# Row norm of the first products applied at their evictions, rotary tables made in place, key halves split step by step

## The reference

```python
xn = rmsnorm(x, norm_mix_g[l])
proj = jnp.einsum('bsd,de->bse', xn, w_in[l])
q_lat, kv_lat, k_rope, dq, dk, dv, gate_pre = jnp.split(proj, split_idx, axis=-1)
...
k_pe = apply_rope(k_rope[:, :, None, :], positions, MLA_ROPE_DIM)
...
o_mla = causal_attention(q_mla, k_mla, v_mla).reshape(B, S, MLA_WIDTH)
dq = apply_rope(dq.reshape(B, S, DIFF_HEADS, 2, DIFF_HEAD_DIM), positions, DIFF_ROT_DIM)
dk = apply_rope(dk.reshape(B, S, DIFF_HEADS, 2, DIFF_HEAD_DIM), positions, DIFF_ROT_DIM)
...
gates = jax.nn.sigmoid(gate_pre + b_gate[l])
```

## Time and profile before

| | before |
|---|---|
| three runs, median (lowest to highest) | 1349.06 us (1348.82 to 1349.18) |
| the profiled execution: its time | 1349.33 us |
| the profiled execution: its span | 1347.6 us |
| mean granted TensorE clock of it | 0.989 |
| PE busy | 1299.9 us, 96% |
| DVE busy | 658.7 us, 49% |
| ACT busy | 536.9 us, 40% |
| POOL busy | 52.4 us, 4% |
| chain that ended last | PE 88%, DVE 6%, ACT 3% |

### The profile page before, as it was taken

How to read it: one execution, slowest core, us unless ns; L and a number is a source line. 1 busy time by engine, 2 the same in 40 slices (tenths; PEclk the granted TensorE clock), 3 DMA queues, 4 the chain that set the end, 5 groups by cost and what they waited for, 6 DMA issues and landing times.

```text
span 1347.6 us, 15769 instructions
## 1 busy us (share of the span) xinstructions
PE 1299.9 (96%) x6231; PEld 1072.3 (80%) x6231; DVE 658.7 (49%) x997; ACT 536.9 (40%) x901; POOL 52.4 (4%) x95
## 2 busy tenths in 40 slices
PE   7999998999999899999999999999999999999997
PEld 5876776887878788888888787888898888888885
DVE  6676567662174433333332337944544435345544
ACT  5335456562333443343421224434563324223222
POOL 0000232121000000000000000000000000000000
PEclk8998999999999999999999999999999999999999
DMA  5223101113153123223232321432113332232221
GB/s 189 55 56 113 32 16 48 48 51 121 48 181 116 63 94 93 93 93 106 82 123 86 118 94 42 130 95 63 33 32 111 102 115 94 94 94 86 88 93 63
DMA packets 104379, 116.39 MB, mean 86 GB/s; under 512 B 13374, under 2 KB 88188, under 8 KB 104316
## 3 DMA queue, kind: packets, MB, share of 16 engines
...
...
## 4 chain that ended last, share of the span: by engine, by line
PE 88%; DVE 6%; ACT 3%; issue 1%; POOL 1%; DMA 0%; SPq 0%; DVEq 0%; ACTq 0%; POOLq 0%
PE ps_mm L1737 56%; PE ps_mm L1772 20%; PE ps_s L1865 2%; PE ps_o L2051 2%; PE ps_o L1887 2%; DVE kd_lo L1311 1%; PE ps_t L2031 1%; DVE w_lo L1054 1%; ACT w_hi L582 1%; ACT tmp L607 1%; PE ps_s L1908 1%; PE ps_t L1875 1%; PE ps_o L1930 1%; PE ps_s L2016 1%; PE ps_s L2014 1%
## 5 line engine op out<-in xcount | busy, mean ns | idle before, releaser
L1737 PE MATMUL ps_mm<-act_hi,w_hi 128*128 128x512 f32 x944 | 372.4, 395 | 2.1 <-DVE w_lo L1063 1.5
L1737 PE MATMUL ps_mm<-act_lo,w_hi 128*128 128x512 f32 x944 | 370.9, 393 | 0.0
L1737 PE MATMUL ps_mm<-act_hi,w_lo 128*128 128x512 f32 x944 | 370.7, 393 | 0.0
L1054 DVE TENSOR_TENSOR w_lo<-stage,w_hi 128x2048 fp32r<-128x2048 f32 (+3 forms) x77 | 157.7, 2049 | 212.5 <-ACT w_hi L582 212.3
L1737 PEld LDWEIGHTS ps_mm<-act_hi,w_hi 128*128 128x128 f32 x944 | 177.8, 188 | 37.8 <-DVE w_lo L1063 1.9
L1737 PEld LDWEIGHTS ps_mm<-act_hi,w_lo 128*128 128x128 f32 x944 | 177.7, 188 | 35.5
L1737 PEld LDWEIGHTS ps_mm<-act_lo,w_hi 128*128 128x128 f32 x944 | 177.9, 188 | 34.6
L582 ACT ACTIVATE w_hi<-stage 128x2048 fp32r<-128x2048 f32 (+3 forms) x78 | 134.1, 1719 | 164.7 <-PE ps_mm L1772 121.8
L1433 DVE TENSOR_TENSOR w_lo<-stage,w_hi 128x2048 fp32r<-128x2048 f32 x23 | 52.7, 2293 | 104.2 <-ACT w_hi L842 104.2
L1772 PE MATMUL ps_mm<-w_hi,act_hi 128*128 128x512 f32 x256 | 100.7, 393 | 1.9 <-issue 1.9
L1772 PE MATMUL ps_mm<-w_hi,act_lo 128*128 128x512 f32 x256 | 100.3, 392 | 0.0
...
## 6 DMA issues: line engine op xcount, KB each, us to landing
...
```

What stands on the lines that cost most here:

```text
L1054: V.tensor_tensor(w_lo[:, s, 0:k * w], stage[:, s, 0:k * w], w_hi[:, s, 0:k * w].bitcast(F32), ALU.subtract).then_inc(w_lo_made, 1)
L1737: ins = T.matmul(ps_mm[:, 2 * bank_slot + m, :], wt[:, kk, m * P:(m + 1) * P], acts[ap][:, kk, :], start=(r == 0), stop=(r == per - 1), sk ...
```

## The change

- **First unit without the row factor.** The tiles of x are transposed as they land, unscaled. Unit 0 comes in four transfers (a quarter of it per column chunk), the first right behind tile 0. Column chunk 0 of each tile is turned into a bank of `ps_mm`, split per tile, and multiplied at once; chunks 1 to 3 follow with all tiles. The gains are loaded by eight transfers from ACT's queue, the first alone is needed at the start. Four matmuls of `keep_warm` stay of twelve.
- **Row factor later.** ACT squares x after the splits; DVE's `rsqrt` comes after the first table. The factor is applied where results leave PSUM: in `keep_latents` (four instructions for unit 2 where there were two), in `dv`'s eviction. For results that are transposed (columns are rows of x), PE makes a row `xr_b` by four transposes of the broadcast factors; POOL multiplies it into both halves of `rope_d`, and DVE multiplies every gate bank by it (`gate_norm`, 16 new instructions), which frees the bank; ACT's tanh then works in place in SBUF.
- **Tables in place.** Angles and sines are computed in the table itself; the last DVE instruction of a table goes, an absolute value on ACT comes. The third table is made in the down projection. The order on ACT and DVE between units 1 and 4 changes.
- **Keys split by steps.** A head's four pieces go to steps 12 to 15, 18 to 21 and 25 to 28 of the MLA loop; the last head's four to step 35.

```diff
+SPLIT_AT = {12 + i: [(0, i)] for i in range(4)}
+SPLIT_AT.update({18 + i: [(1, i)] for i in range(4)})
+SPLIT_AT.update({25 + i: [(2, i)] for i in range(4)})
+SPLIT_AT[MLA_STEPS] = [(3, i) for i in range(4)]
...
+
+                sp.dma_start(slot(stage, 0, k0, w0)[:, kk, :], src0[:, kk, :]).then_inc(first_landed[kk], 16)
+
             for t in range(TT):
                 sp.dma_start(x_in[:, t, :], xv[:, t, :]).then_inc(x_landed[t], 16)
...
-            straight(0)
-            sp.dma_start(freq[:, 0:2], A["rope_freq"]).then_inc(freq_landed, 16)
+                if t == 0:
+                    first_part(0)
+            first_part(1)
+            first_part(2)
+            first_part(3)
+            sp.dma_start(freq, A["rope_freq"]).then_inc(freq_landed, 16)
             sp.dma_start(pos_i[:, :], A["positions"].broadcast_to([P, S])).then_inc(pos_landed, 16)
+            straight(1)
...
+            pool.wait_ge(sincos_made, 2)
+            pool.wait_ge(xr_spread, 1)
+            for i in range(2):
+                linked_after(G.tensor_tensor(rope_d[:, i, :], rope_d[:, i, :], xr_b[:, :], ALU.mult))
...
+            for name, n in ROWS:
+                act.dma_start(rows[ROW0[name]:ROW0[name] + n, :], A[name].rearrange("a (r p) -> (a r) p", p=P)
+                              ).then_inc(rows_landed if ROW0[name] else first_row_landed, 16)
...
+                g = (gates, gates_b)[c // 8][:, c % 8, :]
+                act.wait_ge(bank_free, freed(u, m))
+                nc.scalar.activation(g, g, ACT.Tanh, scale=0.5,
+                                     bias=hcol[:, ROW0["b_gate"] + c:ROW0["b_gate"] + c + 1]).then_inc(gates_made, 1)
...
+            def diff_k_hi(hd, piece):
+
+                e = piece // 2
+                half = (piece % 2) ^ e
                 act.wait_ge(d_roped, hd + 1)
+                act.wait_ge(s_full, 8 * hd + 8)
+                nc.scalar.activation(kd_hi[half * DD:half * DD + DD, 2 * hd + e, :], dk[e * DD:e * DD + DD, hd, :],
+                                     ACT.Copy).then_inc(kd_hi_made, 1)
...
+            act.wait_ge(first_landed[0], 16)
+            nc.scalar.activation(w_hi[:, 0, 0:512], stage[:, 0, 0:512], ACT.Copy)
+            act.wait_ge(cols_made, 1)
             for t in range(TT):
-                act.wait_ge(x_landed[t], 16)
-                squares(x_in[:, t, :], x_sc[:, t, :], ssq[:, t:t + 1], norm_squared)
-            act.wait_ge(rstd_made, 1)
-            scale_tiles(x_sc, x_in)
-            act.wait_ge(cols_made, 1)
...
-                    ins = nc.scalar.activation(w_hi[:, 0, cc], stage[:, 0, cc], ACT.Copy)
+                if t < TT - 1:
+                    act.wait_ge(first_turned, t + 1)
+                else:
+                    act.wait_ge(norm_turned, 1)
+                nc.scalar.activation(act_hi[:, 0, t * P:(t + 1) * P], ps_mm[:, t, 0:P], ACT.Copy,
+                                     scale=col[:, 0:1]).then_inc(first_hi if t < TT - 1 else norm_hi, 1)
...
+            for k in range(1, 4):
+                cc = slice(512 * k, 512 * k + 512)
+                act.wait_ge(first_landed[k], 16)
+                ins = nc.scalar.activation(w_hi[:, 0, cc], stage[:, 0, cc], ACT.Copy)
                 if k == 3:
                     ins.then_inc(w_hi_made, 1)
                 norm_hi_chunk("norm_mix_g", 0, k)
+            norm_hi_chunk("norm_mix_g", 0, 4)
             hi(1)
+            for k in range(5, KD):
+                norm_hi_chunk("norm_mix_g", 0, k)
+            for t in range(TT):
+                if t:
+                    act.wait_ge(norm_squared, t)
+                squares(x_in[:, t, :], tmp[:, :, :].rearrange("p a n -> p (a n)"), ssq[:, 12 + t:13 + t], norm_squared)
...
+            hi(2)
+            for t in range(TT):
+                act.wait_ge(bank_free, freed(1, t))
+                latent_squares(t, t, 0, QR)
+            sincos(0, rope_m)
+            hi(3)
+            for t in range(TT):
+                act.wait_ge(bank_free, freed(2, t // 2))
+                latent_squares(TT + t, t, QR, QR + KVR)
             hi(4)
-
-            act.wait_ge(bank_free, freed(2, 1))
-            for t in range(TT):
-                squares(lat[:, t, 0:QR], tmp[:, 0, 0:QR], ssq[:, t:t + 1], lat_squared)
-                act.wait_ge(lat_squared, 2 * t + 1)
-                squares(lat[:, t, QR:QR + KVR], tmp[:, 0, 0:KVR], ssq[:, 4 + t:5 + t], lat_squared)
-                act.wait_ge(lat_squared, 2 * t + 2)
+            sincos(1, rope_d)
...
+            act.wait_ge(lam_summed, 1)
+            nc.scalar.activation(lexp, lsum, ACT.Exp).then_inc(lam_exp, 1)
...
+                for hd, piece in SPLIT_AT.get(p, ()):
+                    diff_k_hi(hd, piece)
...
+                if i == 2:
+                    sincos(2, rope2)
...
+            V.tensor_copy(col[:, 0:8], ps_mm[:, 3, 0:8]).then_inc(cols_made, 1)
...
+                if t == 0:
+                    V.tensor_tensor(w_lo[:, 0, 0:512], stage[:, 0, 0:512], w_hi[:, 0, 0:512].bitcast(F32), ALU.subtract)
+                tb = slice(t * P, (t + 1) * P)
+                V.scalar_tensor_tensor(out=act_lo[:, 0, tb], in0=ps_mm[:, t, 0:P], scalar=col[:, 0:1],
+                                       in1=act_hi[:, 0, tb].bitcast(F32), op0=ALU.mult, op1=ALU.subtract
+                                       ).then_inc(first_lo if t < TT - 1 else norm_lo, 1)
...
+            dve.wait_ge(norm_squared, TT)
+            rsqrt(TT, 1.0 / D, made=1, c0=12)
...
+                for t in range(TT):
+                    r = rstd[:, 12 + t:13 + t]
+                    if u == 1:
+                        V.tensor_scalar(lat[:, t, 0:512], bank(u, t), r, None, ALU.mult).then_inc(bank_free, 1)
+                    else:
...
             keep_latents(1)
+            dve.wait_ge(xr_turned, 1)
+            V.tensor_copy(xr_b[:, :], ps_o[:, :]).then_inc(xr_spread, 1)
+            angles(rope_d, 1, pos_f[:, :])
             lo(3)
...
+            def gate_norm(u, m, c):
+
+                V.tensor_tensor((gates, gates_b)[c // 8][:, c % 8, :], bank(u, m), xr_b[:, :], ALU.mult
+                                ).then_inc(bank_free, 1)
...
+                dve.wait_ge(gates_made, c + 1)
...
+            for m in range(2):
+                gate_norm(U0["gate_m"], m, m)
+            dve.wait_ge(lam_exp, 1)
...
                 lo(U0["gate_b"] + i + 1)
+                for m in range(2):
+                    gate_norm(U0["gate_b"] + i, m, 8 + 2 * i + m)
...
+                if i == 1:
+                    dve.wait_ge(iota_made, 1)
+                    after(link(V.tensor_copy(rope2[:, 0, :], rope2[:, 0, :].bitcast(I32))))
+                    angles(rope2, 1, rope2[:, 0, :])
...
-            keep_warm(8)
-            pe.wait_ge(ident_made, 1)
-            pe.wait_ge(rows_landed, 16 * len(ROWS))
-            T.transpose(ps_t[:, 0:NROWS], rows[0:NROWS, :], ident[0:NROWS, 0:NROWS]).then_inc(cols_turned, 1)
-            pe.wait_ge(cols_made, 1)
             keep_warm(4)
...
-            wide_unit(0, acts_x, chunk_waits=(norm_lo, 0), w_by_chunk=True)
+            pe.wait_ge(first_row_landed, 16)
+            T.transpose(ps_mm[:, 3, 0:8], rows[0:8, :], ident[0:8, 0:8]).then_inc(cols_turned, 1)
+
+            def turn_x(t, k):
+
+                out = side_bank(k)[:, t * P:(t + 1) * P] if k else ps_mm[:, t, 0:P]
+                return T.transpose(out, x_in[:, t, k * P:(k + 1) * P], ident[:, :])
+
+            def first_products(t, kk):
+
+                for n, (wp, ap) in enumerate(PASSES):
+                    ins = T.matmul(ps_mm[:, t, :], acts_x[ap][:, kk, t * P:(t + 1) * P],
+                                   slot((w_hi, w_lo)[wp], 0, 4, 512)[:, kk, :], start=(kk == 0 and n == 0), stop=False)
+                return ins
+
+            for t in range(TT):
+                pe.wait_ge(x_landed[t], 16)
+                if t == TT - 1:
+                    pe.wait_ge(cols_made, 1)
+                for k in range(4):
+                    ins = turn_x(t, k)
+                    if t == TT - 1:
+                        ins.then_inc(norm_turned, 1)
+                    elif k == 0:
+                        ins.then_inc(first_turned, 1)
+                if t:
+                    pe.wait_ge(first_lo, t)
+                    first_products(t - 1, 0)
+            for kk in range(4):
+                pe.wait_ge(norm_lo, kk + 1)
+                for t in range(TT):
+                    ins = turn_x(t, 4 + kk)
+                ins.then_inc(norm_turned, 1)
+                for t in range(TT):
+                    if kk or t == TT - 1:
+                        ins = first_products(t, kk)
+            ins.then_inc(w_used, 1)
             wide_unit(1, acts_x, chunk_waits=(norm_lo, 0))
+            pe.wait_ge(rows_landed, 16 * (len(ROWS) - 1))
+            T.transpose(ps_s[:, 0, 0:NROWS], rows[0:NROWS, :], ident[0:NROWS, 0:NROWS])
+            pe.wait_ge(rstd_made, 1)
+            for t in range(TT):
```

(2 more changed lines are left out.)

189 lines of the change are left out of this document (86 added, 103 removed).

## The result

| | before | after |
|---|---|---|
| median (lowest to highest) | 1348.94 us (1347.00 to 1349.18), 4 runs | 1330.81 us (1330.31 to 1331.37), 4 runs |
| profiled execution, its span | 1347.6 us | 1329.1 us |
| mean granted clock | 0.989 | 0.995 |
| PE busy | 1299.9 us | 1290.7 us |

The ratio is 0.9869 with a 95% interval of 0.9855 to 0.9883: 18.1 us less, forecast 18.4. That interval is 15.8 to 19.6 us, and in the measurements further down the kernel before has medians from 1346.48 to 1348.85 us, so the gain is known to some 2 us only. To be within 0.3 of it is luck in part, and the terms were not met as exactly as the total.

The account below looks back on a forecast made before the run. PE was busy 96% of the span, so only its idle stretches and clock could give time. Start 12.2 plus seam 8.6, less loop pieces 2.1 and gates 0.3, made 18.4 us: 1330.7 from 1349.06, range 1326 to 1337.

Parts of the forecast that it names:

- Start: From the first transfers to the latents: earlier products and no latents' wait gain 12.2 us, bounds 8.5 and 14.
- I let it reach the upper level near 11: At the start, PE, busy for most of the time since 4.2 us, reaches its faster clock near 11 us.
- the latents are ready at 56.7; the wait of 1.26 goes: Behind units 2 and 3: latents ready at 56.7 us, PE there at 57.2, so its 1.26 us wait disappears.
- Seam: Before the second attention's scores: 8.6 us gained, from waits of 0.62 and 5.63, lower clock 2.0, scores 0.3.
- Rival (e): At the seam something else is late for the second scores and half the wait stays: 1335 us, chance 0.08.
- Pieces in the loop: Twelve key pieces on ACT and DVE in the MLA loop cost 2.1 us, bounds 0 and 8.
- the sum over six steps: MLA loop's piece costs: 0.8 us at `om_lo`, 0.2 in steps 19 and 20, 0.35 and 0.75 in 27 and 28.
- Rival (b): In the MLA loop each piece costs PE its length in all twelve steps, 8 us, not 2.1: 1337 us, chance 0.12.
- Gates: ACT's tanh waits for DVE's eviction of each gate bank: 0.3 us lost for all 16, bounds 0 and 6.
- Rival (d): Each of 16 gates holds ACT, whose next copy comes late; at 1.4 us a gate 1353 us, chance 0.04.
- Third table: In the down projection, 5 us of DVE work hidden in its idle time at no cost; 2 us without that cover.
- Rival (a): PE's clock stays low at the start through unit 0, so the start gives 6 to 8 us: 1336 us, chance 0.14.

Follow-up runs that it names:

- before_warm_seam: The kernel before, with 24 warm-up products ahead of the second attention's second score step: 1346.49 us against 1347.04, ratio 0.9994.
- warm_at_loop: The changed kernel with 3 warm-up products ahead of the MLA loop's third score step and 6 behind it: 1330.02 us, ratio 0.9870 to the kernel before.

## Why the prediction was right, and where it was not

The sum was right in total because errors of both signs met: -2.6 us at the start and -0.5 at the gates, +2.7 in the loop (half of that clock), +0.4 at the seam and +0.2 in the rest.

**Start, 12.2 forecast, 9.59 measured.** The mechanism held: first product at 8.61 us (before 10), unit 2 at 36.46 instead of 46.90. Two terms missed. First, "I let it reach the upper level near 11": it was 12.0 in this execution, and the tiles and chunk 1 came some 0.6 us later than worked out (the wait of 0.75 ends at 15.23, forecast 14.6 after 0.8). So unit 2 came 0.9 us late against the forecast 35.6. This is no error of the sum: in the nine other profiles with the same start unit 2 began at 34.77 to 35.89, where the forecast had it. Second, "the latents are ready at 56.7; the wait of 1.26 goes". They were ready at 60.3, the wait grew to 1.96, a miss of 2 us. The last square ended at 49.3 instead of 47.6, and POOL held DVE for 2.1 us more. The text had priced POOL's pair nowhere at the start, though it had read POOL's effect on DVE in the loop. The warning of the Trainium skill that it cites (SBUF — State Buffer, Who interferes with whom) applied at a place to which it was not put. By the run that moved POOL's work that costs 1.4 us. The forecast had left only 0.5 us of room there (latents at 56.7, PE at 57.2). Within the start no run separates the row factor's move from the new order of the transfers.

**Seam, 8.6 forecast, 8.97 measured** in this pair, 9.0 in the old kernel alone. The mechanism and its four parts are right. The first maximum stands at 218.70 us on DVE and the second scores at 220.39, on time. Rival (e) is refuted.

**Pieces in the loop, 2.1 forecast, 0.74 measured**, twice. The step that failed is the sum over six steps. Only step 15's `om_lo` made a visible wait (0.45, forecast 0.8). The other 0.29 us are spread over the loop, with no wait over 0.2 us to show for it. The `pt` copies of steps 19, 20, 27 and 28 had the slack that the text half denied them. Rival (b) is refuted.

**The loop's clock, not forecast, +1.3.** The changed loop gained 0.56 us although it paid 0.74, since its lower stretch was 3.4 us long and not 6.8. By `before_warm_seam` and `warm_at_loop` such a stretch comes and goes and costs 2.8 and 1.6 us. It is no merit of the change.

**Gates, 0.3 forecast, 0.77 measured**, not in the diff loop, where the text looked, but at the last gate behind it. There ACT's next halves stand behind the tanh. Rival (d) has the mechanism (a gate holds ACT) at a single gate.

**Third table, 0 forecast, 0 measured** in the down projection (61.28 us against 61.32); its leaving the start was worth 4.0 us of wait, counted within the latents' chain. Rival (a) did not occur: unit 0 ran at the upper level from 12 us on, and ended at 24.88.
